# A three-layer transformer block stack with a mixture of experts: work of the stage borders moved, norms turned through the identity, TensorE's expert loop written out

## What is computed

```python
def first_block(x, mem, ...):
    mem_h = rmsnorm(mem, mem_norm)
    for layer in range(2):
        h = rmsnorm(x, mix_norm[layer])
        # memory keys: rmsnorm per head of 64, memory values
        if layer == 0:   # short convolution of gated columns
            y_tok = short_conv_mixer(z[..., :3 * 768], a_conv_w)
        else:            # sparse attention: compressed, selected and window keys
            y_tok = nsa_mixer(q_raw, gate_logits, q_gain, *shared, rel_bias)
        y_mem = memory_attention(q_mem, mem_k, mem_v, mem_q_gain[layer])
        x = x + concat([y_tok, y_mem]) @ w_out[layer]
        hm = rmsnorm(x, mlp_norm[layer])
        x = x + square(relu(hm @ w_up[layer])) @ w_down[layer]      # 1024 -> 4096 -> 1024
        if layer == 0:
            shared = build_shared_kv(x, kv_norm, w_kv_shared, ...)
    return x

def second_block(x, ...):
    h = rmsnorm(x, attn_norm_g)
    proj = h @ w_in                       # 3328 + 5152 + 2048 columns
    y_a, y_b = rwkv7_mix(...), ssd_mix(...)
    x = x + (g_a * (y_a @ w_up_rwkv) + g_b * (y_b @ w_up_ssd)) @ w_out
    h2 = rmsnorm(x, ffn_norm_g)
    x = x + hier_moe(h2, ...)             # 32 experts, top 2 of a group of 8, 1024 -> 512 -> 1024
    return rmsnorm(x, final_norm_g)
```

## Time and profile before

| | |
|---|---|
| median of 3 runs | 1973.81 us (1971.02 to 1975.17) |
| the profiled execution | 1972.69 us, of it span 1970.8 us |
| TensorE | 1708.6 us busy, 87% of the span |
| VectorE, ScalarE, GpSimd | 901.3, 585.4, 38.8 us busy |
| mean granted TensorE clock | 0.919 |
| moved by DMA | 380.49 MB, mean 193 GB/s |

### The profile page before, as it was taken

The page is one execution under the profiler, slowest core; times in us unless marked ns, Lnnn a source line. Parts: engine busy times, 40 slices in busy tenths (PEclk is TensorE's granted clock), DMA queues, the critical chain, the costliest instruction groups (busy, mean ns, idle before and its releaser), DMA issues. The chain is left out here.

```text
span 1970.8 us, 32077 instructions
## 1 busy us (share of the span) xinstructions
PE 1708.6 (87%) x13731; PEld 1270.0 (64%) x13731; DVE 901.3 (46%) x1401; ACT 585.4 (30%) x831; POOL 38.8 (2%) x61
## 2 busy tenths in 40 slices
PE   6877999877779999896987898959779999999995
PEld 3876999754568998795887795547654434344442
DVE  2465555321755553686575585644651211111111
ACT  1424444201544442324102473444321111111110
POOL 2000000000000000001000000000000000000000
PEclk9988999988799999896998898979878999999998
DMA  8403754232017444330000442435077999999993
GB/s 295 171 1 112 275 205 154 85 132 91 1 44 296 173 170 170 129 132 12 3 3 3 171 172 107 150 107 184 30 269 321 427 428 427 426 427 427 427 426 140
DMA packets 101324, 380.49 MB, mean 193 GB/s; under 512 B 9916, under 2 KB 20271, under 8 KB 88139
## 3 DMA queue, kind: packets, MB, share of 16 engines
q1 hardware_dynamic: 99163, 378.03, 49.5%
q10 hardware_dynamic: 1680, 0.43, 0.1%
q0 software_dynamic: 352, 0.15, 0.0%
HBM read 377.45 MB, written 1.14 MB: 192 GB/s over the span
## 5 line engine op out<-in xcount | busy, mean ns | idle before, releaser
L1321 DVE TENSOR_TENSOR mlp_w_lo<-weight_slots,mlp_w_hi 128x2048 fp32r<-128x2048 f32 x64 | 143.8, 2289 | 59.2 <-ACT mlp_w_hi L1291 59.2
L2869 PE MATMUL ps<-weight_slots,moe_h 128*64 128x512 f32 x512 | 148.0, 623 | 9.5 <-issue 6.0
L136 PE MATMUL ps<-mlp_h_hi,mlp_w_hi 128*128 128x256 f32 x512 | 146.4, 286 | 5.6 <-DVE mlp_w_lo L1321 5.6
L137 PE MATMUL ps<-mlp_h_lo,mlp_w_hi 128*128 128x256 f32 x512 | 146.4, 286 | 0.0
L138 PE MATMUL ps<-mlp_h_hi,mlp_w_lo 128*128 128x256 f32 x512 | 146.2, 286 | 0.0
L2869 PE MATMUL ps<-moe_slots,moe_h 128*64 128x512 f32 x512 | 140.9, 593 | 3.2 <-DMA moe_slots<-in_w_exp_up 2.4
L1291 ACT ACTIVATE mlp_w_hi<-weight_slots 128x2048 fp32r<-128x2048 f32 x64 | 119.4, 1910 | 58.1 <-PE ps L138 48.4
L2947 DVE TENSOR_TENSOR moe_hidT<-moe_silu,ps 128x256 f32<-128x256 f32 x32 | 13.5, 421 | 245.2 <-ACT moe_silu L2906 245.2
L136 PEld LDWEIGHTS ps<-mlp_h_hi,mlp_w_hi 128*128 128x128 f32 x512 | 99.6, 195 | 7.8 <-DVE mlp_w_lo L1321 7.2
L2869 PEld LDWEIGHTS ps<-weight_slots,moe_h 128*64 128x64 f32 x512 | 47.1, 144 | 87.9 <-issue 87.9
L137 PEld LDWEIGHTS ps<-mlp_h_lo,mlp_w_hi 128*128 128x128 f32 x512 | 99.7, 195 | 0.5
(11 more groups left out here) (620 smaller groups left out, 4033.8 us busy)
## 6 DMA issues: line engine op xcount, KB each, us to landing
weight_slots<-in_w_in SPq DMA_DIRECT2D x20, 2048.0 KB, 7.9
weight_slots<-in_w_up SPq DMA_DIRECT2D x16, 2048.0 KB, 7.7
weight_slots<-in_w_down SPq DMA_DIRECT2D x16, 2048.0 KB, 7.8
weight_slots<-in_w_exp_gate SPq DMA_DIRECT2D x16, 2048.0 KB, 21.2
weight_slots<-in_w_exp_up SPq DMA_DIRECT2D x16, 2048.0 KB, 19.8
moe_slots<-in_w_exp_up SPq DMA_DIRECT2D x16, 2048.0 KB, 22.1
moe_slots<-in_w_exp_down SPq DMA_DIRECT2D x16, 2048.0 KB, 18.9
moe_slots<-in_w_exp_gate SPq DMA_DIRECT2D x16, 2048.0 KB, 22.4
```

The source lines that it names most:

```text
L136: pe.matmul(dst, left[0], right[0], start=start, stop=False, skip_group_check=inside)
L137: pe.matmul(dst, left[0], right[1], start=False, stop=False, skip_group_check=inside)
L1321: dve.tensor_tensor(piece_slot(w_split[1], jj), raw_piece(jj), piece_slot(w_split[0], jj).bitcast(F32), ALU.subtract).then_inc(w_lo, 1)
L2869: mm = pe.matmul(ps[side(kind), 0, :], h_sel[:, k, :], w[kind][:, k, :], start=(k == 0), stop=(k == KD - 1))
```

## The change

Seven edits in one:

- The gap stands in front of the two `w_out` units, and `prefetch` can run ahead of its stage: both first units of the first MLP are issued in `a_in`, the two others in `out0`; the second MLP's four units in `out1`; the experts' first four in `out2`.
- `out0` and `out1` also split the first two pieces of the MLP behind them, into buffers of their own (`mlp_first`, `split_next`); the MLP finds them ready (`begun`).
- `mlp` begins its sums with products of zeros in bf16 and adds `x` at the end; `close_sums` uses bf16 zeros, and DVE waits bank by bank (also after the experts).
- `norm` scales `x` first (tile 0 by DVE in halves, tile 1 by ACT) and turns it by 16 transposes with the identity.
- `head_norm` takes its root on ACT (`Sqrt`) and a reciprocal on DVE; POOL has no part in it.
- The first piece of a `split_stage` comes in three steps: one chunk, one chunk, two chunks.
- TensorE's list of the experts has no loop: all four trips are written out. The other engines keep theirs.

```diff
-    def prefetch(self, sp, end):
-        while self.issued < min(end + RING, len(self.src)):
+    def prefetch(self, sp, end, ahead=0):
+        while self.issued < min(end + ahead + RING, len(self.src)):
...
-        def gap():
-            while len(stream.src) % RING:
+        def gap(n=0):
+            while (len(stream.src) + n) % RING:
                 stream.src.append(None)
...
+        gap(D // UC)
         plan("out0", *columns(a["w_out"][0], 0, D))
-        gap()
         plan("mlp0", *mlp_units(0))
...
                 def steps(n):
-                    return [slice(0, half_chunks // 2), slice(half_chunks // 2, half_chunks)] if n == 0 \
-                        else [slice(0, half_chunks)]
+                    return [slice(0, 1), slice(1, 2), slice(2, half_chunks)] if n == 0 else [slice(0, half_chunks)]
+                def after(n, s):
+                    return n + 3 if s.stop == half_chunks else s.stop
...
                             if p < n_pieces:
                                 split_w(p, slice(0, half_chunks))
+                        if early and n == len(units) - 1:
+                            split_next()
                         for j in whole[0][n]:
                             empty(j)
...
+                        def split_next():
+                            w, raw, u = early
+                            act.wait_ge(stream.sems[u % RING], stream.need[u])
+                            for j in range(2):
+                                act.activation(w[0][:, j], raw(j), ACT.Copy).then_inc(next_hi, 1)
...
+                        def split_next():
+                            w, raw, u = early
+                            for j in range(2):
+                                dve.wait_ge(next_hi, j + 1)
+                                dve.tensor_tensor(w[1][:, j], raw(j), w[0][:, j].bitcast(F32), ALU.subtract)
...
                     def _(act):
-                        act.activation(squared[:, 0, :], src[:, 0, :], ACT.Square, scale=D ** -0.5,
+                        act.activation(scaled[:, 0, :], src[:, 0, :], ACT.Square, scale=D ** -0.5,
                                        accum_out=stat[:, 0, 0:1]).then_inc(squares, 1)
...
+                        act.wait_ge(rooted, 1)
+                        act.activation(scaled[:, 1, :], src[:, 1, :], ACT.Copy, scale=stat[:, 1, 1:2]).then_inc(scaled_a, 1)
...
                         dve.wait_ge(rooted, 1)
-                        for t in range(NT):
-                            dve.tensor_scalar(diag[:, t, :], ident, stat[:, 1, t:t + 1], None, ALU.mult)\
-                                .then_inc(scale, 1)
...
+                        for h in range(2):
+                            half = slice(h * UC, (h + 1) * UC)
+                            dve.tensor_scalar(scaled[:, 0, half], src[:, 0, half], stat[:, 1, 0:1], None, ALU.mult)\
+                                .then_inc(scaled_v, 1)
...
                         for c in range(KD):
-                            for t in range(NT):
-                                if c == 0:
-                                    pe.wait_ge(scale, t + 1)
-                                mm = pe.matmul(ps[:, c, t * P:(t + 1) * P], src[:, t, c * P:(c + 1) * P], diag[:, t, :],
-                                               start=True, stop=True)
-                            mm.then_inc(turned, 1)
+                            if c % 4 == 0:
+                                pe.wait_ge(scaled_v, c // 4 + 1)
+                            pe.transpose(ps[:, c, 0:P], scaled[:, 0, c * P:(c + 1) * P], ident)
+                        pe.wait_ge(scaled_a, 1)
+                        for c in range(KD):
+                            pe.transpose(ps[:, c, P:S], scaled[:, 1, c * P:(c + 1) * P], ident).then_inc(turned, 1)
...
                     for dst, src, sq, st, g, k in items:
                         act.activation(sq, src, ACT.Square, scale=HD ** -0.5 / k).then_inc(sums, 1)
...
                     for n, (dst, src, sq, st, g, k) in enumerate(items):
-                        pool.wait_ge(means, n + 1)
...
-                        pool.tensor_tensor(st[:, 1], st[:, 0], half, ALU.pow).then_inc(roots, 1)
+                        act.wait_ge(means, 2 * n + 2)
+                        act.activation(st[:, 1], st[:, 0], ACT.Sqrt).then_inc(roots, 1)
...
+                        dve.reciprocal(st[:, 0], st[:, 1]).then_inc(scale, 1)
...
+            nought = c_("noughts").bitcast(BF16)
             for b in range(4, 8):
-                mm = pe.matmul(ps[:, b], c_("noughts")[:, 0:P], c_("noughts"), start=False, stop=True)
+                mm = pe.matmul(ps[:, b], nought[:, 0:P], nought[:, 0:UC], start=False, stop=True)
+                if closed is not None:
+                    mm.then_inc(closed, 1)
...
                         for t in range(NT):
                             for h in range(2):
-                                pe.matmul(acc(t, h), ident, x[:, t, h * UC:(h + 1) * UC], start=True, stop=False)
+                                pe.matmul(acc(t, h), nought[:, 0:P], nought[:, 0:UC], start=True, stop=False)
...
-                        for j in range(SPLIT):
+                        act.activation(begun[:, 0:1], c_("noughts")[0:1, 0:1], ACT.Copy).then_inc(w_hi, 2)
+                        for j in range(2, SPLIT):
                             split(0, j)
...
-                        dve.wait_ge(closed, 1)
                         for t in range(NT):
                             for h in range(2):
-                                dve.tensor_copy(x[:, t, h * UC:(h + 1) * UC], acc(t, h))
+                                dve.wait_ge(closed, 2 * t + h + 1)
+                                part = x[:, t, h * UC:(h + 1) * UC]
+                                dve.tensor_tensor(part, part, acc(t, h), ALU.add)
...
-                        with pe.Fori(0, trips - 1) as i:
+                        for i in range(trips - 1):
                             for b in range(body):
                                 expert(i, b)
```

More of the change, by code:

```diff
@@ L165, in arrived, with load @@
         return self.view(n)
-    def load(self, sp, n):
+    def load(self, sp, n, end):
         src, kc, cols = self.src[n]
         before = [u for u in range(n - RING, -1, -RING) if self.src[u] is not None][:1]
+        assert not before or before[0] < end
         if before and before[0] in self.done:
```

152 lines of the change are left out of this document (83 added, 69 removed).

## The result

The changed kernel takes 1924.48 us (median of 4 runs, 1922.38 to 1925.86) against 1972.99 us of the kernel before: ratio 0.9757, 95% interval 0.9742 to 0.9771. The changed kernel run again gave 0.9765 (0.9749 to 0.978). The profiled execution has a span of 1923.0 us and a mean granted clock of 0.926 (before 0.919).

The account below looks back on a forecast made before the run. TensorE, busy 1708.6 of 1970.8 us, was taken to bound the kernel, with gains where it starts late, waits or delays others. Terms 9.5 + 8.5 + 9.0 + 5.1 + 0.9 - 0.4 = 32.6 gave 1941.2 us, range 1932 to 1949.

Parts of the forecast that it names:

- MLP entry: Start of both MLPs: no identity products or wait for the first split; 4.8 us saved each, 9.5 kept for two.
- Closes: Three ends of sums: bf16 zeros and DVE starting behind the first product save 9.0 us, bounds 5.5 and 9.3.
- Norms over heads: `nsa_q` saves 3.7 us, `mq1` 1.4, `kn` 0 with the root on ACT; together 5.1, bounds 3.0 and 5.5.
- rival price of 2.1: ACT's two added table switches: by a documented drain of 1380 ns each they cost 2.1 us more; no chance given.
- Early splits: `out0` and `out1`: two DVE splits, 4.6 us, fit a hole of about 5; cost nothing, else 1 us each.
- The experts: Experts' stage: DMA load stream is full at 427 GB/s, so removing TensorE's loop gains 0.
- rival B: Experts gain too: 11 us would go if TensorE, not the DMA, set the pace; about 1930; chance 0.06.
- Starts of the split stages: Eight split stages: earlier first product saves 1.2 us in six, 1.0 in two; 8.5 of 9.2 taken, bounds 0 and 9.2.
- the low stretch will come in either case: MLP entry: the 7.55 us from first real product to rectification, partly at low clock, was left unchanged.
- Rival C: A third of the gain given back: late pieces, and earlier starts only move the low clock; gain 22, time 1951; chance 0.15.
- Norms of x: Transposes in all norms of x, less low clock in `kv` (-2.0) and router (-1.0): +0.9 us, bounds -2.5 and +3.9.
- `b_in`: End of `b_in`: the two `w_out` units are issued there, costing 0.4 us at most.

Follow-up runs that it names:

- `u_close`: Changed kernel with the closing products of zeros in float32 again, DVE still waiting bank by bank: 1929.0 us, ratio 0.9788.
- `u_roots`: Changed kernel with the roots of the norms over heads back on POOL (function `head_norm` of before): 1923.11 us, ratio 0.9771.
- `half_loop`: Changed kernel with TensorE's experts loop put back and the experts' loads behind the first eight halved: 1918.16 us, ratio 0.9726.
- `half_unrolled`: Changed kernel, no TensorE loop over the experts, with the experts' loads behind the first eight halved: 1905.45 us, ratio 0.9659.
- `p_steps`: Kernel before with only the three-step first piece of each split stage added: 1948.11 us, ratio 0.9887 to the kernel before.
- `u_norm`: Changed kernel with the function `norm` of before put back, so all norms of x turn by products with diagonals: 1918.85 us, ratio 0.9733.
- `after_again`: The changed kernel run again with nothing altered: 1924.77 us, ratio 0.9765.
- `delay1`: Changed kernel with an added stage ahead of `n4` in which DVE makes one copy: 1919.26 us, ratio 0.9738.
- `delay2`: Changed kernel with an added stage ahead of `n4` in which DVE makes two copies: 1927.28 us, ratio 0.9761.
- `warm_rw`: Changed kernel with 40 bf16 products of zeros on TensorE at the beginning of its 13 us wait in `rwkv`: 1922.62 us, ratio 0.9755.
- `mixed`: Changed kernel with the norms of the two MLPs and `n2` by diagonals as before, `n4` and `n5` by transposes: 1921.61 us, ratio 0.9747.
- `warm`: Changed kernel with 18 bf16 products of zeros on TensorE in every norm of x while it waits for the scaled halves: 1918.64 us, ratio 0.9736.

## Why the prediction was wrong

**Right.** TensorE's ends and starts bound the kernel. MLP entry: 9.4 of 9.5, but the closeness is luck: the entries gave 5.7 and 5.8 where I had 4.75 each, and the loop behind it took 1.1 back, which I had not foreseen. Closes: 9.1 of 9.0, `u_close` showing two equal halves. Norms over heads: 5.5 of 5.1 by their borders, though the total of `u_roots` doesn't show them; no drain (its rival price of 2.1 is nowhere). Early splits: hidden in `out0` and `out1`, as said. The experts: DMA-bound as the earlier trace rows said, rival B refused rightly, and its 11 us shown where they would be (`half_loop` less `half_unrolled`, 10.4).

Of the 15.2 us by which the sum fell short (47.8 against 32.6), the starts of the split stages are 4.6, the norms of x 3.0, and places that the sum did not have 7.4.

**The step that failed** is "Starts of the split stages": 8.5 of at most 9.2, and with it the sentence on the MLPs, "the low stretch will come in either case". I took the low clock as a fixed stretch behind the first product, and weighed only whether the second piece would be late. The earlier first product was right to a tenth (1.71 and 1.41 us). But with the earlier first product the clock also stayed up or rose sooner: TensorE's idle time in front of it fell from 3.6 to 5.1 us to 2.4 to 3.9, the mean clock of these stretches went from 0.69 to between 0.74 and 0.84, and the term is 13.1 in the changed kernel, 15.8 alone; taken out, it costs 11 to 13 us. The upper bound, 9.2, was no bound but nearly the lower end: over sixteen traces the eight starts gave 9.7 to 15.8. I had also argued that with the clock full at once the wait for the second piece would eat the gain. That wait comes (0.77 us in `out1`, 0.64 in `rwkv_in` of `p_steps`), but these starts gained 2.4 and about 3 us, because the same starts before ran at 0.50 for some 6 us. Whether it is the shorter idle time or the pattern of smaller first steps that keeps the clock up was not separated. I had read the clock in `out0` alone, which with `gate` is one of two stages at 0.83 over their first 10 us; the six others stand at 0.66 or 0.57, so there was more to win than `out0` shows.

**Missing in the sum.** 7.4 us. The sum put every stretch without an edit at nothing, without a reason. The experts' start is 2 us shorter when TensorE's loop is gone, by eighteen traces; of the rest the larger pieces, the router's end and nsa's attention, are stretches with the same instructions and no edit. Their mean clock was higher (the router's end 0.66 where it was 0.57, the attention 0.77 where it was 0.74); what raised it there isn't shown. Rival C had the sign of this wrong: starting earlier does not only move the low clock, in 68 of 128 starts it came with a higher one.

**Norms of x.** Forecast 0.9, by borders 3.9, within the bounds; in time the sign cannot be told, as `u_norm` is 5 to 6 us under the changed kernel while its trace is 6.4 us shorter than that of `after_again` in `rwkv` alone. The price of the clock behind transposes, 1.4 in `kv` and 1.2 in the router, was near the 2.0 and 1.0 taken. The row read for the norm's products, 390 to 392 in the earlier trace rows, lies behind the last of them (389.4); in `n2` they ran at 0.50 from 386 to 388 and at 0.99 in the next two microseconds.

**Open.** The loop of the MLP is 0.16 us slower per pair of units in every kernel built on the changed one, also without early splits, and not in `p_steps`. The products of 512 columns take 395 ns there at the median and 389 before; why was not found. `b_in` lost 1.3 where I had 0.4; of it 0.8 lies between its last job and `nsa_q` and was not tested. Why the loop of the experts lengthens the low clock before its first turn isn't known either. What the whole is worth apart from the clock can't be given as one number: the six edits taken out singly cost about 12 (steps), 5 (closes), 2 (roots), 2 (early splits), 4 (loop) and -5 us (norms) by their times, some 20 of 48. The zeros at the MLPs' start and the earlier loads were not taken out by themselves.

## What to carry to other kernels

Where a border leaves TensorE idle for 3.6 to 5.1 us, as here, cutting that by 1.0 to 1.2 us was worth 0.6 to 1.3 us where the clock came out the same and 1.75 to 3.5 where it came out higher; cost such a border with the clock of that stretch in both states, and not with the one seen. Judge an edit by the borders that it touches and by several kernels' traces; its total contains stretches that move by up to 8 us on their own, so that singly undone edits don't add up. TensorE's turns of a loop cost nothing here while a full DMA set the pace, and 10.4 us for two as soon as it didn't.

## What the runs showed of the hardware

- A kernel with a stage of 1.1 us put in was 5 us faster than the one without (`delay1` 0.9738 against 0.9765, intervals just touching; 7.5 us between the profiled executions), and the traces differ by the granted clock in one stretch of `rwkv`: 200.3 us or 208. Two copies in place of one (`delay2`, 208.5) did not do it.
- That stretch took 208.1 to 208.7 us in eleven traces, 200.3 to 201.9 in five, and 203.5 and 205.8 in one each. Some kernels repeat their total from run to run (`warm_rw` 1922.4 to 1923.4, `mixed` 1921.4 to 1923.0), others don't (`u_roots` 1920.9 to 1930.4).
- Products of zeros held the clock at 1.00 while they ran (`warm`, `warm_rw`). In `warm_rw` they ended 4.7 us before the next products, and the clock was at 0.50 when these began.
- A table load of 1.28 us was followed at once by the next activation where that had nothing to wait for (`kn`: 423.77 + 1.28, then 425.06).
